# One hybrid decoder trunk: the layer loop written out on every engine, waits on constants

## The reference

```python
def decoder_layer(x, l, ...):
    x = x + 0.5 * swiglu(rms_norm(x, ffn1_norm[l]), ffn1_w_gu[l], ffn1_w_down[l])
    h = rms_norm(x, mix_norm[l]);  z = h @ w_in[l]
    # A: sparse attention (compressed, selected and window branch)
    # B: gated DeltaNet (short convolution, delta rule in chunks)
    # C: HGRN2 (forget gates, outer-product states, in chunks)
    merged = sum(sigmoid(m_g[i]) * (branch[i] @ w_branch[l, i]) for i in range(3))
    x = x + merged @ w_out[l]
    x = x + 0.5 * swiglu(rms_norm(x, ffn2_norm[l]), ffn2_w_gu[l], ffn2_w_down[l])
    return x, new caches and states
```

## Time and profile before

| | |
|---|---|
| median of 3 runs | 3571.92 us (3569.67 to 3580.83) |
| the profiled execution | 3584.17 us, its span 3582.3 us |
| PE busy | 90% of the span, 28132 matmuls |
| DVE, ACT, POOL busy | 31%, 31%, 34% |
| mean granted clock of TensorE | 0.918 of 2.4 GHz |
| DMA | 283.38 MB, 79 GB/s |
| code fetched by the queues of kind instruction | 150 packets with 2.46 MB, 63 with 0.52 MB |

### The profile page before, as it was taken

The page is one execution under the profiler, slowest core; times in us unless marked ns, Lnnn a source line. Parts: engine busy times, 40 slices in busy tenths (PEclk is TensorE's granted clock), DMA queues, the critical chain, the costliest instruction groups (busy, mean ns, idle before and its releaser), DMA issues.

```text
span 3582.3 us, 70606 instructions
## 1 busy us (share of the span) xinstructions
PE 3238.9 (90%) x28132; PEld 2796.5 (78%) x28132; DVE 1107.7 (31%) x1877; ACT 1118.4 (31%) x1826; POOL 1215.4 (34%) x776
## 2 busy tenths in 40 slices
PE   6999897897977998999989998978889779989999
PEld 6888785587866887888878887855778678878887
DVE  3221203354254224321132212034543541252211
ACT  4332322441331323332233323234313313233322
POOL 2434311333152343343434343123322513333434
PEclk9999986998888899999999999769889979999999
DMA  4343310120121222223323333101101112322223
GB/s 142 108 150 91 117 62 1 44 77 2 48 76 50 72 95 95 82 95 95 100 88 131 124 93 118 50 1 56 66 2 54 70 50 79 105 77 94 97 92 116
DMA packets 87655, 283.38 MB, mean 79 GB/s; under 512 B 13330, under 2 KB 26514, under 8 KB 84882
## 3 DMA queue, kind: packets, MB, share of 16 engines
q1 hardware_dynamic: 87298, 278.54, 23.6%
q10 hardware_dynamic: 144, 1.86, 0.1%
HBM read 265.28 MB, written 15.09 MB: 78 GB/s over the span
## 4 chain that ended last, share of the span: by engine, by line
issue 53%; PE 21%; POOL 20%; DVE 3%; POOLq 1%; ACT 1%; DMA 1%; DVEq 0%; ACTq 0%; SPq 0%
POOL w_lo L1948 17%; PE pair L1958 8%; PE pair L249 2%; PE pair L386 1%; PE pair L349 1%; PE pair L360 1%; POOL mixed L1615 1%; PE pair L298 1%; PE pair L335 1%; PE pair L103 1%; POOL mixed L1616 1%; PE pair L701 1%; POOL arena L1615 1%; PE pair L1025 1%; POOLq L2438 1%
## 5 line engine op out<-in xcount | busy, mean ns | idle before, releaser
L1948 POOL TENSOR_TENSOR w_lo<-raw,w_hi 128x1024 f16<-128x1024 f32 x452 | 986.8, 2194 | 1909.9 <-ACT w_hi L1944 1909.9
L1958 PE MATMUL pair<-h_hi,w_hi 128*128 128x260 f16 x2752 | 772.1, 281 | 34.0 <-ACT arena L1685 17.6
L1958 PE MATMUL pair<-h_lo,w_hi 128*128 128x260 f16 x2752 | 768.6, 279 | 0.0
L1958 PE MATMUL pair<-h_hi,w_lo 128*128 128x260 f16 x2752 | 768.4, 279 | 0.0
L1967 PE MATMUL pair<-arena,w_hi 128*128 128x260 f16 x4096 | 699.7, 278 | 28.8 <-DVE arena L2376 16.8
L1944 ACT ACTIVATE w_hi<-raw 128x1024 f16<-128x1024 f32 x452 | 464.8, 1053 | 580.6 <-PE pair L1967 394.5
L1967 PE MATMUL pair<-h_hi,w_hi 128*128 128x260 f16 x2176 | 598.2, 275 | 3.6 <-DVE mixed L735 3.6
L1967 PE MATMUL pair<-h_hi,w_lo 128*128 128x260 f16 x2176 | 598.0, 275 | 0.0
L1967 PE MATMUL pair<-h_lo,w_hi 128*128 128x260 f16 x2176 | 598.0, 275 | 0.0
L1967 PE MATMUL pair<-arena,w_lo 128*128 128x260 f16 x2048 | 568.6, 278 | 0.0
L1967 PEld LDWEIGHTS pair<-arena,w_hi 128*128 128x128 f16 x4096 | 404.4, 99 | 90.7 <-POOL w_lo L1948 17.9
(11 more groups left out here) (383 smaller groups left out, 3533.9 us busy)
## 6 DMA issues: line engine op xcount, KB each, us to landing
raw<-in_w_up SPq DMA_DIRECT2D x180, 512.0 KB, 3.2
raw<-in_w_z SPq DMA_DIRECT2D x84, 512.0 KB, 3.3
raw<-in_w_dn SPq DMA_DIRECT2D x64, 512.0 KB, 3.5
raw<-in_w_mg SPq DMA_DIRECT2D x48, 512.0 KB, 3.4
raw<-in_w_dn SPq DMA_DIRECT2D x32, 384.0 KB, 3.1
raw<-in_w_wb SPq DMA_DIRECT2D x24, 512.0 KB, 3.2
raw<-in_w_out SPq DMA_DIRECT2D x16, 512.0 KB, 3.3
arena<-in_slc_pages SPq DMA_DIRECT2D x32, 128.0 KB, 2.8
```

The source lines that it names most:

```text
L1948: e.tensor_tensor(w_lo[s % 4], raw[s % 2], w_hi[s % 4], ALU.subtract).then_inc(w_split, 1)
L1958: mm = pe.matmul(out, w[s % 4][:, k, :], xx[:, k, a * HALF:(a + 1) * HALF], start=(k == 0 and p == 0), stop=(k == KD - 1 and p == 2))
```

## The change

`for l in range(L)` takes the place of `with engine.Fori(0, L) as l` on all five engines. So l is a number of the program's text: each engine's program holds both layers one behind the other, the branch back to the layer's head is gone, and every number that depends on l alone is a constant. The inner loops stay loops, now two of each where there was one, and what depends on r is still worked out in registers.

```diff
-            with sp.Fori(0, L) as l:
+            for l in range(L):
...
-            with pe.Fori(0, L) as l:
+            for l in range(L):
...
-            with act_e.Fori(0, L) as l:
+            for l in range(L):
...
-            with dve.Fori(0, L) as l:
+            for l in range(L):
                 dve.tensor_copy(vec[:, :], vecs[:, bass.DynSlice(l * NVEC, NVEC)])
...
-            with pool.Fori(0, L) as l:
+            for l in range(L):
```

## The result

The changed kernel took **3555.78 us**, median of 6 executions (3553.34 to 3562.05); the kernel before, beside it on the same chip, 3571.85 (6 executions). The ratio is **0.9957, 95% interval 0.9943 to 0.9971**: 15 us faster. Timed again with more executions of before it was 3554.86 and 0.9945 (0.9929 to 0.9960), so 15 to 20 us. I had said 3565, between 3557 and 3573, and "within 0.3%" as the likeliest.

What follows compares the result with a forecast made beforehand. TensorE, busy 90% of the span, was taken as the bound, with gains only where it runs dry: 4.4 + 0.4 + 2.0 = 6.8 us off the median 3571.92 gives 3565 us, range 3557 to 3573.

Steps and rivals of the forecast that it cites:

- Part 1: Entry into layer 1: without the branch back, VectorE's reciprocal comes 3.9 us sooner; 4.4 us gained (3.9 to 4.8).
- Rival A: Entry into layer 1: VectorE's fetch stall stays in straight code, so 3570 to 3572 us; chance 0.13.
- Part 2: SyncE's stores and weight load after the delta states' write-back: constant addresses save 0.4 us in both layers (0 to 0.6).
- the lower end that I had named: SyncE's weight load: gain 0, as its issue may not set its landing, 8.2 us later behind the stores.
- Part 3: Mixer hand-overs: waits on constants replace register sums, 1.0 us a layer, 2.0 us in both (-0.8 to 8).
- the sum itself: Whole kernel: 4.4 + 0.4 + 2.0 = 6.8 us gained, taken off the profiled time, then off the median.
- the 12 us between the profiled execution and the median: Whole kernel: median 3571.92 us lies 12 us below the profiled 3584.17; the same difference was assumed after the change.
- Rival B: Mixer hand-overs: every register sum counts, total gain 12 to 14 us, so 3558 to 3560 us; chance 0.16.
- my own sign for it: Mixers: one losing over 3 us would show that every register sum counts and the forecast is wrong.
- Rival C: Inner loops: back edges cost 3.6 us instead of 0.208, 34 us on one TensorE loop; with unnamed slowdowns 0.07.

Runs made afterwards that it cites:

- the outlier: One execution, 3610 us at clock 0.895, of the changed kernel with six memsets ahead of its first norm; that program's median 3564.09 us, ratio 0.9981.

## Why the prediction was wrong, step by step

*Part 1, the back edge: right.* Forecast 4.4 us (3.9 to 4.8). The reciprocal is 3.93 us nearer to the sums, the stage lost 4.94, of them 3.8 idle time, and sums kept with the branch gone gave 3 to 4 at equal clock. Rival A is refuted: DVE's copy follows the last branch of the loop at L2386 with 0.27 us of idle time.

*Part 2, SP's addresses: too high.* Forecast 0.4 us. From the first of the four stores to the weight load SP took 2.11 us before and 1.94 after; ACT and PE hardly moved:

```profile
1027.78 1.06 ACT L1944 ACTIVATE w_hi<-raw 128x1024 f16<-128x1024 f32 x1 [20.68 <-DMA raw<-in_w_mg]
1029.42 0.38 PE L1958 MATMUL pair<-h_hi,w_hi 128*128 128x260 f16 x1 [8.73 <-issue]
```

20.77 and 8.78 in the earlier trace rows: 0.1 us. From the load's issue to ACT's start it took 8.20 us before and 8.41 after, so the earlier issue gave nothing, the lower end that I had named.

*Part 3, waits on constants: its 2.0 us not resolved, the price of a clock missing.* Forecast 2.0 us (-0.8 to 8). In the chain of waits between 785 and 847 us, which answers to the earlier trace rows,

```profile
by line: PE pair L1025 7.0%; PE pair L981 6.9%; PE pair L1015 6.6%; PE pair L1027 6.2%; PE pair L982 5.7%; issue 5.6%; PE pair L970 5.6%; DVE arena L1419 5.5%; PE pair L1004 5.1%; PE pair L972 4.8%; PE pair L993 4.3%; PE pair L994 3.4%; DVE
```

"issue" halved, 7.0 us to 3.5. By the whole kernel PE's idle time fell by 7.5 and 6.0 us in the two profiles, which leaves 2 to 3.5 us behind the boundary's 4. The sum of my parts, 6.8 us, is about the idle time that went, but part 3's share of it may be luck. PE's idle time in the two mixers together was 259.2 us before and 256.3 and 257.9 in the changed kernel; it was 257.1 with both layers written out and every sum kept. Single profiles scatter by as much as the part is worth.

*The step that failed is the sum itself.* "So many us less idle, so many us less time" holds only if PE's busy time stays, and I carried the 12 us between the profiled execution and the median over to the forecast as a constant. PE's busy time fell by 14.9 us in one profile and 26.0 in the other, at the same matmuls, as the granted clock rose from 0.918 to 0.924 and 0.927. The clock columns of the earlier trace rows, 0.87 and 0.88 in the mixers, were read and given no term. By the runs it is worth some 10 us of the 15 to 20 here; among the 19 programs its mean moved by up to 0.006, 12 us, and from execution to execution of the kernel before by 0.009. My range had no room for it.

*Rival B* (every register sum counts, 12 to 14 us) names nearly the time that came, and my own sign for it, a mixer that loses over 3 us, was there. Its cause is another: what the mixers lost is busy time and not hand-overs, and twice the register work on three engines cost 2 us at equal clock, within the error. *Rival C* is refuted. The inner branches that answer to the earlier trace rows:

```profile
L2100 PEldq COMPARE_BRANCH  x44: 76/215/235, 54.0 to 3425.4; - x44
L2386 DVEq COMPARE_BRANCH  x24: 50/56/72, 310.4 to 3558.2; - x24
```

*Shown:* that the clock's part does not shrink as the sums get longer, and that beginning both kernels 3 us later takes most of it away. *Not settled:* why before's mean clock is lower. It varies from execution to execution, and yet its mean differs between programs. Before's is at the low end of all that ran and the changed kernel's near the high end, so any variant of either is likely to come out nearer the middle. But luck need not be all. The six programs with every sum in registers on all engines have mean clocks of 0.9205 to 0.9236, the four with every layer number a constant 0.9245 (without the outlier) to 0.9265, and the two groups do not overlap. The constants may have a part of their own in the clock; no run here gives its size or its way. In the single profiles most of the difference lies in attention and the delta mixer, where PE has many short pauses.

## What to carry to other kernels

Where TensorE spends a sixth of the time at its lower clock, a change of half a per cent can be in good part the clock's; read the granted clock of each execution beside its time, and time both kernels once more with their start moved by a few us before a small gain is believed. A layer loop's back edge stalled PE, ACT and DVE here for 3.3 to 4.3 us each, and it counted only on the engine that was late there. Register sums before waits, 32 to 40 ns each, were nearly all covered: the change took the register work of PE, ACT and DVE from 219 to 99 us, and PE's idle time fell by 6.0 to 7.5.

## What the runs showed of the hardware

Of one program, executions differed by 4 to 22 us (before, the most often timed: 3565 to 3587), most of it along one line, 2 us for 0.001 of mean clock. A taken branch back over a whole layer's code stalled PE 3.4 to 3.9, ACT 3.3 and DVE 3.7 to 4.3 us, and DVE a second time by 2 us in four of seven programs. A program without any branch on four engines, 28132 matmuls in a row, took 3552.70 us with 332.9 us of PE's idle time, so it paid nothing for its length. A longer sum before a wait took 83 ns in the middle on PE and ACT and 104 on DVE.
